# Four weight tiles of two output projections: plain fp32 products in place of three products of high and low parts

## The chip, the cores and the metric

The kernel runs on one core of one Trainium2 chip. The metric is the device time of one execution in microseconds (us), and the lower the better. The time before is the median of three runs.

## What is computed

The reference is a stack of two blocks of two layers on an input of 256 tokens by 1024 features, all in fp32. The first block is a banded attention, an MLP, a recurrent (RG-LRU) layer and an MLP. The second is an RWKV-7 time mix and a differential attention. Each of the layers of the second block ends in the same way, and this ending is where the change is:

```python
# layer 0: y is the time mix, layer 1: y is the differential attention
y = y.reshape(B, S, D).astype(xn.dtype) * jax.nn.silu(g)
return y @ w_out                       # w_out is 1024 x 1024: the output projection
...
h = h + rms_norm(y, norm_post[i])
e = p[i] @ ple_w[i]
g = jax.nn.sigmoid(h @ ple_gate[i])
h = h + rms_norm(g * e, ple_norm[i])   # called the embedding step below
```

## The kernel before

**Weights.** All weights are laid out as 73 tiles of 512 columns (or rows), and each tile is four pieces of 128 x 1024 fp32 (512 KB). SP loads the 292 pieces in order into a ring of eight slots (`ring`, line 687); piece m waits until TensorE has used piece m - 8, and TensorE counts the pieces that it has used in `piece_used`. The four tiles of the change are `W_OUT_A`, `W_OUT_A + 1` (pieces 220 to 227) and `W_OUT_B`, `W_OUT_B + 1` (pieces 272 to 279). Behind each pair come the tile of the embedding weights (`W_PLE0` or `W_PLE1`, four plain pieces) and the two gate tiles (eight pieces, split), pieces 232 to 239 and 284 to 291.

**Split products.** Most tiles are multiplied in the reduced fp32r type with a correction. ScalarE rounds the piece to `high_r` (`split_until`, line 868), GpSimd subtracts that from the piece and writes `ring_r` (`low_until`, line 709), and the activations are split in the same way: they are transposed on TensorE into PSUM, ScalarE writes `x_high` (`evacuate_high`, line 268) and VectorE writes `x_low` (`evacuate_low`, line 286). A product of a 128 x 128 and a 128 x 512 block is then three matmuls (high by high, high by low, low by high). The set `PLAIN` names the tiles that are not split. Their product is one fp32 matmul from `ring` itself. The eight tiles of `W_RKVG`, ahead of `W_OUT_A`, are plain already, and so are the two tiles of the embedding weights. Both kinds of product are recorded under line 409.

**Order.** Every engine's program is one hand-written list. `pe_linear` runs a pair of tiles: per tile four pieces, per piece two k blocks by two token tiles, so 16 products a tile and 32 a pair. `hold_clock(bank, n)` (line 203) issues n dummy fp32 matmuls of 128 columns. On ScalarE `split_for(n)` means that all pieces up to 4n + 9 have been split, so ScalarE runs six pieces ahead of the tile at hand, and waits in its program where such a piece has not landed yet. On GpSimd `low_until(4 * W_PLE0)` comes ahead of five DMAs (the embedding inputs pT, four rows of parameters) and that of `lamb` (lines 778, 715 and 782). In the loop over the sixteen heads of the differential attention, ScalarE splits one piece a head (two at the last): from head 10 on these are the pieces of `W_OUT_B`. GpSimd splits them in between its `combine` steps (line 813) and `gate_rows` (line 821).

**The ending of a layer.** TensorE transposes the gated output (instance `T_YA` or `T_OB`), multiplies it with the pair of tiles, and issues 6 dummy matmuls. Then it waits for the squares of the second half (ScalarE, line 1102) and the products with the gain (VectorE, line 1639). It multiplies with the embedding weights (line 2148), transposes h, waits for ScalarE's copy of the embedding (line 1120), issues 9 dummy matmuls and starts the gate tiles. In ScalarE's `out_norm`, `split_for(first + c)` stands ahead of the squares of half c.

Of the kernel before, what the change touches and what calls it, by code (L numbers as in the profile page):

```python
# [14 lines left out]
SEQ, D = 256, 1024  # L15
NT, KT = SEQ // P, D // P
# [8 lines left out]
W_RKVG, W_OUT_A, W_PLE0, W_KVQG, W_OUT_B, W_PLE1, W_TILES = 47, 55, 57, 60, 68, 70, 73  # L25
# [2 lines left out]

REC = ["x0", "x1", "x2", "x3", "x4", "x5", "g0", "x6", "x7", "g1", "y0", "y1", "g2", "g3", "y2", "y3", "y4", "y5", "y6", "y7"]
REC_AT = {name: 4 * W_REC + i for i, name in enumerate(REC)}  # L30
PLAIN = {W_PLE0, W_PLE1} | set(range(W_RKVG, W_RKVG + 8))
PLAIN_PIECES = {REC_AT[f"g{i}"] for i in range(4)} | {4 * n + i for n in PLAIN for i in range(4)}

MLP_TILES = set(range(W_MLP0, W_MLP0 + 16)) | set(range(W_MLP1, W_MLP1 + 16))
# [51 lines left out]
def build(nc, x, w, cols, rows, consts, relt, lora1, lora2, pT, lam, out):  # L86
    with ExitStack() as ctx:
# [3 lines left out]
        def sem(name):  # L91
            return ctx.enter_context(nc.semaphore(name))
# [24 lines left out]
        def shaped(v, dims):  # L117
            if len(dims) < 2:
                return v
            names = "abcd"[:len(dims)]  # L120
            return v.rearrange("p (" + " ".join(names) + ") -> p " + " ".join(names),
                               **{k: d for k, d in zip(names[1:], dims[1:])})

        def view(off, *dims):

            n = int(np.prod(dims))
            assert off + n <= ARENA, (off, dims)
            return shaped(arena[:, off:off + n], dims)

        def place_r(name, off, n):  # L130

            assert off + n <= ARENA
            return nc.alloc_sbuf_tensor_at(name, [P, n], F32R, offset=arena_base + 4 * off, align_bytes=32)[:, :]

        def raw(m, *dims):

            return shaped(ring[:, m % RING, :], dims)
# [4 lines left out]
        def read(v):  # L142

            return v.bitcast(F32)
# [11 lines left out]
        S = 2048  # L156
# [22 lines left out]

        SPLIT_T = {T_H0, T_O, T_H1, T_N2, T_H3, T_YA, T_H6, T_H7, T_OB, T_H8}
        BANK_OF, ACT_BANKS, DVE_BANKS, PREVIOUS, _last = [], [0], [0], [], {}
        for _i in range(T_H8 + 1):
            for _b in range(4):
                bank_ = 4 + _b if _i in SPLIT_T else 3 if _i in (T_K, T_QB) else 6 + _b % 2
                BANK_OF.append(bank_)
                PREVIOUS.append(_last.get(bank_))
                _last[bank_] = len(BANK_OF) - 1
                ACT_BANKS.append(ACT_BANKS[-1] + (_i in SPLIT_T or _b % 2 == 0))  # L190
                DVE_BANKS.append(DVE_BANKS[-1] + (_i in SPLIT_T or _b % 2 == 1))

        def bank_out(eng, g):

            if ACT_BANKS[g + 1]:
                eng.wait_ge(tp_act, ACT_BANKS[g + 1])
            if DVE_BANKS[g + 1]:
                eng.wait_ge(tp_dve, DVE_BANKS[g + 1])
# [41 lines left out]
        def filling(g):  # L240
            return psum[:, BANK_OF[g], :].rearrange("p (j t) -> p j t", j=2)

        def evacuate(eng, inst, b, dst, gain=None):

            g = 4 * inst + b
            eng.wait_ge(tp_filled, g + 1)
            on_act = b % 2 == 0
            assert on_act == (eng is engines["act"])
            if gain is None:
                dd = dst[:, 2 * b:2 * b + 2, :]  # L250
                ins = nc.scalar.copy(dd, filling(g)) if on_act else nc.vector.tensor_copy(dd, filling(g))
            else:
                for j in range(2):
                    k = 2 * b + j
                    if on_act:
                        ins = nc.scalar.activation(dst[:, k, :], filling(g)[:, j, :], ACT.Copy, scale=gain[:, k:k + 1])
                    else:
                        ins = nc.vector.tensor_scalar(dst[:, k, :], filling(g)[:, j, :], gain[:, k:k + 1], None, ALU.mult)
            ins.then_inc(tp_act if on_act else tp_dve, 1)

        def evacuate_high(act, inst, *pairs, between=None):

            for b in range(4):
                g = 4 * inst + b
                act.wait_ge(tp_filled, g + 1)
                for dst, gain in pairs:
                    if gain is None:
                        ins = nc.scalar.copy(dst[:, 2 * b:2 * b + 2, :], filling(g))
                    else:
                        for j in range(2):  # L270
                            k = 2 * b + j
                            ins = nc.scalar.activation(dst[:, k, :], filling(g)[:, j, :], ACT.Copy, scale=gain[:, k:k + 1])  # L272
                ins.then_inc(tp_act, 1)
                if between is not None:
                    between(b)

        def evacuate_low(dve, inst, *triples):

            for b in range(4):
                g = 4 * inst + b  # L280

                dve.wait_ge(tp_act, ACT_BANKS[g + 1])
                for hi, dst, gain in triples:
                    if gain is None:
                        u = slice(2 * b, 2 * b + 2)
                        ins = nc.vector.tensor_tensor(dst[:, u, :], filling(g), read(hi[:, u, :]), ALU.subtract)
                    else:
                        for j in range(2):
                            k = 2 * b + j
                            ins = nc.vector.scalar_tensor_tensor(out=dst[:, k, :], in0=filling(g)[:, j, :],  # L290
                                                                 scalar=gain[:, k:k + 1], in1=read(hi[:, k, :]),
                                                                 op0=ALU.mult, op1=ALU.subtract)
                ins.then_inc(tp_dve, 1)
# [5 lines left out]
        def h_halves(pe, n):  # L299
# [37 lines left out]
        kv_act, kv_dve, roped, lam_sum, lam_exp, comb_ready, o_act, o_sq, o_var, o_root, od_ready, o_taken, rd_ready, b_scaled = (  # L337
            sem(n) for n in ("kv_act", "kv_dve", "roped", "lam_sum", "lam_exp", "comb_ready", "o_act", "o_sq", "o_var",
                             "o_root", "od_ready", "o_taken", "rd_ready", "b_scaled"))
# [12 lines left out]
        XH, XL, XBH, XBL = (shaped(place_r(name, at * S, S), (KT, SEQ)) for name, at in  # L352
                            (("x_high", 10), ("x_low", 11), ("xb_high", 6), ("xb_low", 7)))
        xT2, xTb2 = (XH, XL), (XBH, XBL)

        def junk_at(i):
            return view((5 if i < 6 else 8) * S, NT, D)
# [35 lines left out]
        def transposed(pe, inst):  # L393

            return lambda i: bank_out(pe, 4 * inst + i)

        def pe_piece(pe, n, i, bank, lhs):

            m = 4 * n + i
            for t in range(NT):  # L400
                tt = slice(t * P, (t + 1) * P)
                for j in range(2):
                    k = 2 * i + j
                    if n in PLAIN:
                        pairs = ((lhs[:, k, tt], raw(m, 2, HALF)[:, j, :]),)
# [7 lines left out]
        def pe_chunk(pe, n, c, lhs, banks_free, ready=None):  # L413

            for i in range(4):
                piece_ready(pe, 4 * n + i)
                if ready is not None:

                    ready(i)
                if i == 0 and banks_free is not None:  # L420
                    banks_free(pe, c)
                pe_piece(pe, n, i, 2 * (c % 2), lhs)

        def pe_linear(pe, first, chunks, lhs, banks_free=None, ready=None):
            for c in range(chunks):
                pe_chunk(pe, first + c, c, lhs, banks_free, ready if c == 0 else None)
# [409 lines left out]
        def _(act):  # L836
# [293 lines left out]
                        square_half(ge[:, t, hl], c, t, 2 * e_n + 1)  # L1130
                post_root(i)

            evacuate_high(act, T_YA, (XH, None))
            out_norm(6, W_OUT_A, 0)
            embed(7, W_PLE0, 0, T_H6)

# [37 lines left out]
            for hh in range(HEADS + 2):  # L1174
# [25 lines left out]
                if hh in PAIR_AT2:  # L1200
                    i, which, b = PAIR_AT2[hh][0]
# [8 lines left out]
                    nc.scalar.copy(pt2[:, g % 2, :], psum[:, 6 + g % 2, 0:384]).then_inc(pt_copied, 1)  # L1210
            heads_square(1)
            heads_root(1)
            evacuate_high(act, T_OB, (XH, None))
            out_norm(9, W_OUT_B, 1)
            embed(10, W_PLE1, 1, T_H8)

# [2 lines left out]
        def _(dve):  # L1219
# [36 lines left out]
            for hh in range(HEADS + 3):  # L1256
# [13 lines left out]
                if hh in PAIR_AT and PAIR_AT[hh][0] % 2 == 1:  # L1270
                    i, which, b = PAIR_AT[hh]
# [381 lines left out]
                                                   g_[:, hl].unsqueeze(1).broadcast_to([P, NT, HALF]), ALU.mult))  # L1653
                add_normed(i, 2 * e_n + 1)

            evacuate_low(dve, T_YA, (XH, XL, None))
            out_gain(6, W_OUT_A, 0, "norm_post0")
            dve.wait_ge(h_ready, 6)
            embed_dve(7, 0, T_H6, "ple_norm0")
# [49 lines left out]
            for hh in range(HEADS + 1):  # L1709
# [18 lines left out]
                if hh in PAIR_AT2:  # L1728
                    i, which, b = PAIR_AT2[hh][1]
# [8 lines left out]
            heads_var(1)  # L1738
            heads_norm(1)
            heads_gate(1)  # L1740
            evacuate_low(dve, T_OB, (XH, XL, None))
            out_gain(9, W_OUT_B, 1, "norm_post1")
            dve.wait_ge(h_ready, 8)
            embed_dve(10, 1, T_H8, "ple_norm1")
# [3 lines left out]
        def _(pe):  # L1748
# [32 lines left out]
            for hh in range(HEADS + 3):  # L1781
# [7 lines left out]
                if hh in PAIR_AT:  # L1789

                    i, which, b = PAIR_AT[hh]
# [363 lines left out]

            pe_transposes(pe, T_YA, yN, lambda b: pe.wait_ge(y_ready, b // 2 + 1))
            hold_clock(0, 8)
            pe_linear(pe, W_OUT_A, 2, xT2, None, transposed(pe, T_YA))
            embed_pe(W_PLE0, 0, T_H6)


# [77 lines left out]
            kvqg_out(8)  # L2239
            hold_clock(0, 16)  # L2240
            pe_transposes(pe, T_OB, oD, lambda b: pe.wait_ge(od_ready, b // 2 + 1))
            pe_linear(pe, W_OUT_B, 2, xT2, lambda pe, c: pe.wait_ge(o_taken, 2) if c == 1 else None, transposed(pe, T_OB))
            embed_pe(W_PLE1, 1, T_H8)

def layout(inp):
# [101 lines left out]
```

## Time and profile before

| | before |
|---|---|
| median of 3 runs | 1169.71 us (1169.52 to 1169.93) |
| the profiled execution | 1173.79 us, span 1172.0 us |
| TensorE matmul busy | 1113.3 us, 95% of the span |
| ScalarE busy | 540.0 us, 46% |
| GpSimd busy | 707.8 us, 60% |
| VectorE busy | 475.7 us, 41% |
| mean granted clock of TensorE | 0.988 of full speed |

All steps below are read in the one profiled execution, whose span runs from its first to its last instruction. A time such as 884.16 is that instruction's start in us from the start of the span. A matmul's record is longer than the distance to the next one, since matmuls are pipelined: the cost of one is the distance between starts.

### The profile page before, as it was taken

Reading aid. Unit: us, or ns where it says so; the run is one execution under the profiler, and the core shown is the slowest. Engines: PE = TensorE matmul, PEld = TensorE weight load, DVE = VectorE, ACT = ScalarE, POOL = GpSimd, SP = SyncE. Lnnn points to the kernel's source line nnn. Section 1 sums busy time; section 2 is a strip of 40 time slices with the busy share of each in tenths; the row PEclk is TensorE's granted clock in tenths of the full one; section 3 lists DMA queues with packets and bytes.
Section 4 is the critical chain, followed back from the end, with each engine's and each line's share of the span. In section 5 each row is a group of like instructions: output and inputs, shape, how many; then the busy total and the mean of one; then the engine's idle time right before and its main releaser. Section 6 shows DMA issues by size and latency. Waiting matters only on the chain. (4 is left out here: it accounts for less than half of the span.)

```text
span 1172.0 us, 20965 instructions
## 1 busy us (share of the span) xinstructions
PE 1113.3 (95%) x8956; PEld 925.5 (79%) x8956; DVE 475.7 (41%) x647; ACT 540.0 (46%) x851; POOL 707.8 (60%) x443
## 2 busy tenths in 40 slices
PE   9999999999999899999999999899998889999895
PEld 8788799998899789989984445899847677777864
DVE  1125274333246646521137175535641350233332
ACT  6437364444458755544421151212222564559452
POOL 5975459988947599998820035300034849667770
PEclk9999999999999999999999998999999989999998
DMA  8661455555546355555572443000036425433240
GB/s 319 225 233 55 144 159 184 189 188 189 189 129 212 110 162 183 191 186 193 183 233 72 127 158 110 21 4 4 4 127 236 150 95 183 140 100 120 81 159 36
DMA packets 45852, 169.44 MB, mean 145 GB/s; under 512 B 5088, under 2 KB 5344, under 8 KB 45440
## 3 DMA queue, kind: packets, MB, share of 16 engines
q1 hardware_dynamic: 43312, 159.06, 41.3%
q0 software_dynamic: 2448, 9.05, 2.4%
q8 instruction: 71, 1.16, 0.4%
q14 instruction: 21, 0.17, 0.0%
HBM read 167.03 MB, written 1.05 MB: 143 GB/s over the span
## 5 line engine op out<-in xcount | busy, mean ns | idle before, releaser
L709 POOL TENSOR_TENSOR ring_r<-ring,high_r 128x512 fp32r<-128x512 f32 (+1 forms) x368 | 636.6, 1763 | 238.9 <-ACT high_r L868 223.8
L868 ACT CAST high_r<-ring 128x1024 fp32r<-128x1024 f32 x248 | 256.2, 1049 | 215.6 <-DMA ring<-w 213.5
L435 PE MATMUL psum<-x_high,high_r 128*128 128x256 f32 x640 | 182.4, 285 | 2.2 <-DVE x_low L290 2.2
L435 PE MATMUL psum<-x_low,high_r 128*128 128x256 f32 x640 | 181.1, 283 | 0.0
L435 PE MATMUL psum<-x_high,ring_r 128*128 128x256 f32 x640 | 181.1, 283 | 0.0
L409 PE MATMUL psum<-high_r,x_high 128*128 128x512 f32 x320 | 127.3, 398 | 2.5 <-POOL ring_r L709 1.5
L612 DVE TENSOR_TENSOR arena<-arena 128x512 f32<-128x512 f32 x32 | 54.8, 1713 | 179.6 <-ACT arena L588 179.5
L435 PEld LDWEIGHTS psum<-x_high,high_r 128*128 128x128 f32 x640 | 122.7, 192 | 3.5 <-issue 1.8
L409 PE MATMUL psum<-high_r,x_low 128*128 128x512 f32 x320 | 124.8, 390 | 0.0
L409 PE MATMUL psum<-ring_r,x_high 128*128 128x512 f32 x320 | 124.6, 389 | 0.0
L435 PEld LDWEIGHTS psum<-x_low,high_r 128*128 128x128 f32 x640 | 122.7, 192 | 0.5
L435 PEld LDWEIGHTS psum<-x_high,ring_r 128*128 128x128 f32 x640 | 122.7, 192 | 0.0
L409 PE MATMUL psum<-ring,arena 128*128 128x512 f32 x256 | 115.2, 607 | 0.0
L654 PE MATMUL psum<-high_r,zz_high 128*128 128x512 f32 x256 | 99.8, 390 | 1.3 <-DVE zz_low L619 1.3
L654 PE MATMUL psum<-ring_r,zz_high 128*128 128x512 f32 x256 | 99.7, 390 | 0.0
L654 PE MATMUL psum<-high_r,zz_low 128*128 128x512 f32 x256 | 99.6, 389 | 0.0
L409 PEld LDWEIGHTS psum<-ring,arena 128*128 128x128 f32 x256 | 49.0, 194 | 60.3 <-issue 60.1
L409 PEld LDWEIGHTS psum<-high_r,x_high 128*128 128x128 f32 x320 | 60.0, 188 | 16.4 <-ACT x_high L272 1.6
L409 PEld LDWEIGHTS psum<-high_r,x_low 128*128 128x128 f32 x320 | 60.1, 188 | 12.9
L409 PEld LDWEIGHTS psum<-ring_r,x_high 128*128 128x128 f32 x320 | 60.1, 188 | 11.8
L203 PE MATMUL psum<-con 128*128 128x128 f32 x500 | 59.4, 276 | 5.0 <-ACT arena L1120 3.2
L203 PEld LDWEIGHTS psum<-con 128*128 128x128 f32 x500 | 57.7, 192 | 6.5 <-ACT arena L1120 3.7
(317 smaller groups left out, 1717.2 us busy)
## 6 DMA issues: line engine op xcount, KB each, us to landing
ring<-w SPq DMA_DIRECT2D x292, 512.0 KB, 3.4
row<-rows POOLq DMA_DIRECT2D x14, 512.0 KB, 7.1
arena<-relt SPq DMA_DIRECT2D x2, 1536.0 KB, 10.6
h<-x SPq DMA_DIRECT2D x1, 1024.0 KB, 5.0
arena<-lora POOLq DMA_DIRECT2D x2, 512.0 KB, 6.8
out<-h SPq DMA_DIRECT2D x1, 1024.0 KB, 4.0
con<-consts SPq DMA_DIRECT2D x1, 529.0 KB, 4.5
arena<-pT POOLq DMA_DIRECT2D x2, 256.0 KB, 4.8
```

The source lines that it names most:

```text
L203: nc.tensor.matmul(psum[:, bank, 0:P], sq, sq, start=True, stop=True)
L409: ins = nc.tensor.matmul(psum[:, bank + t, :], a, b, start=(k == 0 and q == 0), stop=(k == KT - 1 and q == len(pairs) - 1))
L435: ins = nc.tensor.matmul(out, a, b, start=(k == 0 and q == 0), stop=(k == KT - 1 and q == 2))
L612: nc.vector.tensor_tensor(zz[:, u, :], zr[:, u, :], zr[:, u, :], ALU.mult).then_inc(zz_ready, 1)
L654: ins = nc.tensor.matmul(psum[:, 2 * t + half, :], a, b, start=(c == 0 and f == 0 and q == 0), stop=(c == 7 and f == 3 and q == 2))
L709: ins = nc.gpsimd.tensor_tensor(low(m)[:, part], raw(m)[:, part], read(high(m))[:, part], ALU.subtract)
L868: nc.scalar.copy(high(m), raw(m)).then_inc(high_made, 1)
```

## The change

The four tiles join `PLAIN`. Their pieces are no longer split by ScalarE and GpSimd, and each of their products is one fp32 matmul in place of three fp32r ones. The transposed activations `T_YA` and `T_OB` are not split either: ScalarE copies banks 0 and 2, VectorE banks 1 and 3, into `xT_full`, an fp32 view of the memory of `x_high`. The PSUM banks stay as they were.

```diff
-PLAIN = {W_PLE0, W_PLE1} | set(range(W_RKVG, W_RKVG + 8))
+PLAIN = {W_PLE0, W_PLE1} | set(range(W_RKVG, W_OUT_A + 2)) | {W_OUT_B, W_OUT_B + 1}
...
-        SPLIT_T = {T_H0, T_O, T_H1, T_N2, T_H3, T_YA, T_H6, T_H7, T_OB, T_H8}
+        SPLIT_T = {T_H0, T_O, T_H1, T_N2, T_H3, T_H6, T_H7, T_H8}
...
-                bank_ = 4 + _b if _i in SPLIT_T else 3 if _i in (T_K, T_QB) else 6 + _b % 2
+                bank_ = 4 + _b if _i in SPLIT_T | {T_YA, T_OB} else 3 if _i in (T_K, T_QB) else 6 + _b % 2
...
+        xT_full = view(10 * S, KT, SEQ)
...
-            evacuate_high(act, T_YA, (XH, None))
+            for b in (0, 2):
+                evacuate(act, T_YA, b, xT_full)
...
-            evacuate_low(dve, T_YA, (XH, XL, None))
+            for b in (1, 3):
+                evacuate(dve, T_YA, b, xT_full)
...
-            pe_linear(pe, W_OUT_A, 2, xT2, None, transposed(pe, T_YA))
+            pe_linear(pe, W_OUT_A, 2, xT_full, None, transposed(pe, T_YA))
```

The same three edits (ScalarE, VectorE, TensorE) are made for `T_OB` and `W_OUT_B`.

## Rows read from the trace of the kernel before

**Rows 1.** Page, part 1 and part 5: busy us, share, instructions; groups under line 409.

```profile
PE 1113.3 (95%) x8956; PEld 925.5 (79%) x8956; DVE 475.7 (41%) x647; ACT 540.0 (46%) x851; POOL 707.8 (60%) x443
...
L409 PE MATMUL psum<-high_r,x_high 128*128 128x512 f32 x320 | 127.3, 398 | 2.5 <-POOL ring_r L709 1.5
...
L409 PE MATMUL psum<-ring,arena 128*128 128x512 f32 x256 | 115.2, 607 | 0.0
```

**Rows 2.** Timeline of TensorE, plain tiles: start us, us, instruction, count, idle before.

```profile
620.27 13.90 PE L409 MATMUL psum<-ring,arena 128*128 128x512 f32 x32
634.10 7.12 PE L1912 MATMUL psum<-arena 128*64 128x256 f32 x32
...
857.11 20.87 PE L409 MATMUL psum<-ring,arena 128*128 128x512 f32 x48
877.81 1.04 PE L215 MATMUL psum<-con,arena 128*128 128x128 f32 x8
```

**Rows 3.** Timeline of TensorE, the pair W_OUT_A: dummies, first products, end.

```profile
881.39 1.95 PE L203 MATMUL psum<-con 128*128 128x128 f32 x16
884.16 0.47 PE L409 MATMUL psum<-high_r,x_high 128*128 128x512 f32 x1 [0.82 <-DVE x_low L286]
...
906.03 1.50 PE L203 MATMUL psum<-con 128*128 128x128 f32 x12
```

**Rows 4.** Timeline of ScalarE and VectorE at the entry of W_OUT_A.

```profile
878.93 3.87 ACT L868 CAST high_r<-ring 128x1024 fp32r<-128x1024 f32 x4
882.71 2.05 ACT L268 CAST x_high<-psum 128x512 fp32r<-128x512 f32 x4
```

**Rows 5.** Timeline of ScalarE and TensorE, from W_OUT_A's end to the gate tiles.

```profile
906.59 1.04 ACT L868 CAST high_r<-ring 128x1024 fp32r<-128x1024 f32 x1 [9.76 <-DMA ring<-w]
907.82 1.04 ACT L868 CAST high_r<-ring 128x1024 fp32r<-128x1024 f32 x1 [0.19 <-DMA ring<-w]
908.77 0.59 ACT L1102 ACTIVATE arena<-psum 128x512 f32<-128x512 f32 x1
...
910.28 8.80 PE L2148 MATMUL psum<-ring,arena 128*128 128x512 f32 x16 [2.75 <-ACT arena L1102]
...
924.07 0.48 PE L409 MATMUL psum<-high_r,x_high 128*128 128x512 f32 x1
```

**Rows 6.** Timeline, the same stretch behind W_OUT_B.

```profile
1122.61 1.50 PE L203 MATMUL psum<-con 128*128 128x128 f32 x12
1122.81 0.60 ACT L1102 ACTIVATE arena<-psum 128x512 f32<-128x512 f32 x1 [0.99 <-PE psum L409]
1124.32 7.11 PE L2148 MATMUL psum<-ring,arena 128*128 128x512 f32 x16 [0.21 <-ACT arena L1102]
1132.29 1.05 ACT L868 CAST high_r<-ring 128x1024 fp32r<-128x1024 f32 x1 [1.72 <-DMA ring<-w]
1137.24 0.48 PE L409 MATMUL psum<-high_r,x_high 128*128 128x512 f32 x1
```

**Rows 7.** Timeline of GpSimd during W_OUT_A: splits, then the DMAs behind them.

```profile
880.04 10.22 POOL L709 TENSOR_TENSOR ring_r<-ring,high_r 128x512 fp32r<-128x512 f32 x8 [0.72 <-ACT high_r L868]
890.22 0.59 POOL L778 DMA_DIRECT2D arena<-pT  x1
890.81 2.09 POOL L715 DMA_DIRECT2D row<-rows  x4
```

**Rows 8.** Windows: busy us (count) of PE, PEld, DVE, ACT, POOL; granted clock; DMA share; GB/s.

```profile
884.00:888.00 4.00, 3.84 (x17) 3.22 (x18) 1.81 (x4) 0.75 (x2) 4.00 (x5) 1.00 0.00 0
...
900.00:904.00 4.00, 4.00 (x20) 3.30 (x19) 0.00 (x0) 0.00 (x0) 0.00 (x0) 1.00 1.03 411
...
912.00:916.00 4.00, 4.00 (x7) 1.55 (x7) 3.69 (x5) 2.09 (x4) 2.72 (x3) 0.63 0.38 131
```

**Rows 9.** Timeline at the last heads of the attention: TensorE, ScalarE and GpSimd.

```profile
1083.41 6.86 PE L203 MATMUL psum<-con 128*128 128x128 f32 x60
1086.73 2.01 ACT L868 CAST high_r<-ring 128x1024 fp32r<-128x1024 f32 x2
1090.54 0.99 POOL L813 TENSOR_TENSOR arena<-arena 128x384 f32<-128x384 f32 x1 [2.34 <-ACT arena L1187]
1091.59 0.55 PE L2237 MATMUL psum<-con,arena 128*128 128x128 f32 x3 [1.31 <-POOL arena L813]
```

**Rows 10.** Chain that ended last, attention, four products of one piece (start us, us, what).

```profile
1058.40 2.95 PE psum L409 x12
```

More of the change, by code:

```diff
@@ L1212, in _ @@
             heads_root(1)
-            evacuate_high(act, T_OB, (XH, None))
+            for b in (0, 2):
+                evacuate(act, T_OB, b, xT_full)
             out_norm(9, W_OUT_B, 1)
@@ L1740, in _ @@
             heads_gate(1)
-            evacuate_low(dve, T_OB, (XH, XL, None))
+            for b in (1, 3):
+                evacuate(dve, T_OB, b, xT_full)
             out_gain(9, W_OUT_B, 1, "norm_post1")
@@ L2241, in _ @@
             pe_transposes(pe, T_OB, oD, lambda b: pe.wait_ge(od_ready, b // 2 + 1))
-            pe_linear(pe, W_OUT_B, 2, xT2, lambda pe, c: pe.wait_ge(o_taken, 2) if c == 1 else None, transposed(pe, T_OB))
+            pe_linear(pe, W_OUT_B, 2, xT_full, lambda pe, c: pe.wait_ge(o_taken, 2) if c == 1 else None, transposed(pe, T_OB))
             embed_pe(W_PLE1, 1, T_H8)
```

## The prediction

> **What bounds the kernel now.** I read the page's busy shares first: TensorE is busy for 1113.3 of 1172.0 us, every other engine for 60% or less [rows 1]. So a change counts by what it does to TensorE's own stretches and to the few holes between them. I then read the timeline of TensorE over the two pairs of tiles, for the distance between starts and not for the mean of a record. The pair W_OUT_A runs from 884.16 to 906.03, 21.87 us for 96 records without a hole [rows 3], 0.228 us a record. It is bound by TensorE alone. The holes lie around it: 0.82 us ahead of the first product, 2.75 us behind the last [rows 3, 5], and one of 1.31 us at the last heads of the attention [rows 9].
>
> **What one product costs, split and plain.** A split product is three records, 21.87 / 32 = 0.683 us. For a plain one the eight W_RKVG tiles are the measure. The group of plain products has 256 records [rows 1], but eight tiles of 16 products are 128: each plain product leaves two records. The timeline says the same: the first W_RKVG tile, 16 products, stands as 32 records from 620.27 to 634.10, and 24 products stand as 48 records from 857.11 to 877.81 [rows 2]. That is 0.864 and 0.863 us a product. The weights come from the same ring and the activations from SBUF, so I take 0.863 us and no other bound is needed; a mean record of 607 ns [rows 1] is neither the cost of a product nor of a record.
>
> The change is therefore 0.863 - 0.683 = 0.180 us more a product, 32 x 0.863 = 27.6 in place of 21.87 us a pair: +5.7 us for each of two pairs, +11.5 us in all. All of it is on the path, since nothing else is late there.
>
> A sentence on the pages: the Trainium skill, Perfetto Trace Analysis, section Engine Utilization, halves the array's output rate for FP32_LOW_HIGH. Read as the price of a whole fp32 product that would be half a plain price, and the change would gain. The page FP8 and Floating Point Precision, section TensorE Precision Notes, names four passes for true fp32, and the trace agrees with this one: two records for a product, each about twice as long in its distance (0.43 us) as an fp32r record (0.228 us).
>
> **What goes away around the pairs.**
>
> *Entry of W_OUT_A.* ScalarE splits four pieces until 882.8 and only then writes x_high [rows 4]; VectorE's x_low follows, and TensorE, whose dummies end at 883.34 (881.39 + 1.95), starts at 884.16 [rows 3]. Now ScalarE is free at 878.93, copies bank 0 at once, and the products start with the end of the dummies: -0.8 us. The dummies themselves stay. The new copies of VectorE (banks 1 and 3) are needed one and three pieces later, 3.5 us and more, and cost nothing. If they were late they would cost at most the 0.8 us again.
>
> *Entry of W_OUT_B.* No hole stands there, the products follow the transposes. Nothing is gained: 0.
>
> *Behind W_OUT_A.* ScalarE must split pieces 232 and 233 ahead of the squares of the second half. They landed late: the first cast starts at 906.59 and the second at 907.82, each after a wait for the DMA, and the squares at 908.77 [rows 5]; behind W_OUT_B they start 0.2 us after the last product [rows 6]. Why late: GpSimd splits until 890.2 and only then issues pT and four rows [rows 7]. The DMA engines stood still at 884 to 888 and were full (share 1.03) at 900 to 904 [rows 8]. Now GpSimd has no piece to split there, so it issues these DMAs about 10 us earlier, when the engines are idle; the queue of the pieces is passed by them in a quiet stretch. The pieces also have more time: slot 232 comes free with the fifth piece of the pair and the last product is 3 x 3.45 us behind it, against 3 x 2.73 us. So the squares should start at once, as behind W_OUT_B. The hole also cost clock: in the stretch 912 to 916 the granted clock is 0.63, between the levels of 1.2 and 2.4 GHz, after TensorE had stood for 2.75 us, and the 16 records of the embedding took 8.80 us, against 7.11 us behind W_OUT_B, where the idle time was 0.21 us [rows 5, 6, 8]. From the start of the six dummies to the first gate product it took 924.07 - 906.03 = 18.0 us [rows 5] and behind W_OUT_B 1137.24 - 1122.61 = 14.6 us [rows 6]. I take the second for both: -3.4 us. What is late next is the cast of the last piece that ScalarE splits ahead of its copy of the embedding (1132.29, after a DMA [rows 6]), which both endings have and which doesn't move against the last product. The bounds of this term: 0 if the transfers are as late as before, and -3.6 us if a little more of the second ending's own wait goes too.
>
> *Behind W_OUT_B.* Its two early pieces have the same extra time and caused no wait: 0.
>
> *The last heads.* Eight casts of about 1.0 us leave ScalarE's list from head 10 on, two of them at 1086.73 just ahead of the scaling for which GpSimd's last combine waits [rows 9], and GpSimd loses 16 half pieces of about 1.3 us (10.22 us for eight [rows 7]). TensorE waits 1.31 us for that combine. But ahead of it TensorE has its own 60 dummy records from 1083.41 to 1090.27 (1083.41 + 6.86), and these don't shrink. So of some 8 us that ScalarE saves, 1091.59 - 1090.27 = 1.3 us reach the path: -1.3 us. The bounds are 0 and -2.8 us. The second is for products that were themselves slightly held up: four split products of a piece stand as 2.95 us in the chain [rows 10], where 12 x 0.228 is 2.74 us, which is 0.2 us for each of about seven such heads, 1.5 us in all.
>
> *Elsewhere.* Behind both gate pairs each engine stands as before relative to TensorE: with eight slots in the ring no splitting engine can run further ahead than it does. The two x_low buffers and the casts that go save time on engines that don't bound.
>
> **The sum**, made in the profiled execution: +5.7 + 5.7 - 0.8 - 3.4 - 1.3 = +5.9 us, so 1179.7 us where it took 1173.8. The median of the runs is 4.1 us below that execution, and the trace can't say which waits are shorter in an unprofiled run; I add the same difference to it: 1169.7 + 5.9 = 1175.6 us. If the wait behind W_OUT_A is one of those that were shorter, its term shrinks and the time is higher, so the upper side of the range is the longer one.
>
> **The rivals.**
>
> *The late pieces stay late* (slower still). The DMAs of GpSimd move, but they may meet the transfers of pieces 224 to 227, and what was a queue at 900 could stay one. Then nothing of the 3.4 us comes back: +9.3 us, 1179.0 us. For it: the transfers were issued in the same order before. Against it: the idle stretch at 884 to 888 [rows 8]. Chance 0.16.
>
> *ScalarE was the real bound of the attention* (not slower). The chain that ended last runs through ScalarE from about 1062 to 1090. If TensorE's products there were held back by it and not only lengthened by restarts, the eight casts could come back in full: 8 us in place of 1.3, and the sum would be -0.8 us, 1168.9 us. The place is heads 10 to 15, the price 1.0 us a cast, and it decides once more than 3.6 of the 8 us reach TensorE (5.9 - 2.3). Against it: TensorE shows no wait there up to 1083.41, and the 60 dummies stand between. Chance 0.06, of which 0.04 stays within 0.2%.
>
> *A record is a product* (the change does what its price would promise). Then a pair takes 13.8 us, -8.1 us each, and with the other terms 1169.7 - 16.1 - 5.5 = 1148 us. The counts of rows 1 and 2 speak against it. Chance 0.01.
>
> *A smaller gain is missed*: the other terms come back more than I take, as by the -2.8 us at the heads and the whole of -3.6 us, or a wait appears at a new place, an entry above all. That spans +3.9 to +7.5 us around my sum, and counts as my forecast; a further 0.05 lies at +1.5 to +3 us by several of them together.
>
> **How the numbers follow.** The forecast has 0.72, its own range 1173.6 to 1177.5 us. The range for 8 in 10 takes in the late pieces with a little of their spread: 1173.0 to 1179.6 us. A measurement of this kernel tells about 0.2% (2.3 us) from no change, so slower by more than that begins at 1172.0 us. Slower: 0.72 + 0.16 + most of the rest, 0.90. Within 0.2%: 0.07, from ScalarE as the bound and from several small gains together. Faster: 0.03.
>
> **What would show it.** In the profile of the changed kernel each pair stands as 64 records over 27.6 us; at half of that the third rival is right. The first product of W_OUT_A starts right behind the dummies. The squares behind it start within half a microsecond of the last product, the embedding's 16 records take about 7.1 us at a granted clock of 1.0, and the stretch to the gate tiles is 14.6 us; where it is 18, the late pieces stayed late. The idle time ahead of the last transposes of the attention is gone, and the 60 dummies are followed at once. The prediction is wrong if the stretch from head 10 to the dummies shrinks by more than 2 us, or if a wait appears inside a pair.

## The result, and the profile after

The changed kernel takes 1176.26 us (median of 4 runs, 1174.55 to 1177.11), beside 1169.82 us before: a ratio of 1.0050, with a 95% interval of 1.0033 to 1.0068. Timed again later (e10 below) it is 1176.41 beside 1171.82 us, 1.0042 (1.0026 to 1.0057). So it is slower by about 5 us, 0.4 to 0.5%. The forecast was 1175.6 us, +5.9 us.

The profiled execution took 1175.56 us, span 1173.8 us, where that of before had a span of 1172.0 us. The spans differ by only 1.8 us, and that is misleading: the changed stretch begins with the dummies ahead of W_OUT_A, and they stand at 881.39 in the trace of before [rows 3] and at 878.11 in that of after. Up to there nothing was changed but ScalarE's and GpSimd's splits of W_OUT_A's first pieces and the start of GpSimd's DMAs (pT at 875.11 in place of 890.22, the rows at 877.42 in place of 890.81). In the fourteen traces of this study that point lies anywhere from 876.3 to 881.4. So each stretch below is compared by itself, from landmark to landmark.

Timeline of TensorE after, W_OUT_A to the gate tiles (columns as in [rows 2]; the line numbers of after are 1 to 5 higher):

```profile
878.11 1.95 PE L203 MATMUL psum<-con 128*128 128x128 f32 x16
879.89 10.46 PE L410 MATMUL psum<-ring,arena 128*128 128x512 f32 x24
...
907.36 1.50 PE L203 MATMUL psum<-con 128*128 128x128 f32 x12
909.08 7.11 PE L2153 MATMUL psum<-ring,arena 128*128 128x512 f32 x16 [0.21 <-ACT arena L1103]
...
919.76 3.65 PE L203 MATMUL psum<-con 128*128 128x128 f32 x18 [1.83 <-ACT arena L1121]
...
923.07 0.77 PE L410 MATMUL psum<-high_r,x_high 128*128 128x512 f32 x1
```

The products run from 879.89 to 907.36, 27.47 us, in place of 21.87 [rows 3]. They start 1.78 us behind the start of the dummies, as soon as these end, in place of 2.77. Behind them the embedding starts after 1.72 us, with 0.21 us of idle time, in place of 4.25 us and 2.75 [rows 5]. Then something new: the 18 dummy records ahead of the gate tiles take 3.65 us, not the 2.27 us that they take where the clock is full. The windows of this stretch show the granted clock (columns as in [rows 8]):

```profile
918.00:920.00 2.00, 0.24 (x2) 0.24 (x3) 0.00 (x0) 2.00 (x3) 2.00 (x2) 1.00 0.74 254
920.00:922.00 2.00, 2.00 (x13) 2.00 (x13) 1.70 (x3) 2.00 (x5) 2.00 (x3) 0.60 0.04 14
922.00:924.00 2.00, 2.00 (x10) 1.86 (x10) 0.79 (x2) 1.55 (x2) 2.00 (x3) 0.55 0.00 0
924.00:926.00 2.00, 2.00 (x10) 1.66 (x9) 0.00 (x0) 0.00 (x0) 2.00 (x3) 1.00 0.02 4
```

TensorE stood still for 1.83 us up to 919.76, and for the next four microseconds it has little more than half of its clock: the level of 1.2 GHz, and then 2.4 GHz again.

ScalarE behind W_OUT_A, after: both casts of the early pieces (232 and 233) are done 2.1 us ahead of the last product, and the squares follow it by 0.2 us.

```profile
900.45 1.05 ACT L869 CAST high_r<-ring 128x1024 fp32r<-128x1024 f32 x1 [5.13 <-DMA ring<-w]
904.24 1.04 ACT L869 CAST high_r<-ring 128x1024 fp32r<-128x1024 f32 x1 [2.74 <-DMA ring<-w]
907.56 0.60 ACT L1103 ACTIVATE arena<-psum 128x512 f32<-128x512 f32 x1 [2.28 <-PE psum L410]
```

The last heads, after, TensorE, GpSimd and VectorE:

```profile
1082.15 6.86 PE L203 MATMUL psum<-con 128*128 128x128 f32 x60
...
1085.38 0.99 POOL L814 TENSOR_TENSOR arena<-arena 128x384 f32<-128x384 f32 x1 [5.89 <-ACT arena L1189]
...
1096.42 1.09 PE L215 MATMUL psum<-con,arena 128*128 128x128 f32 x8 [1.12 <-DVE arena L1710]
...
1095.14 1.22 DVE L1710 SCALAR_TENSOR_TENSOR arena<-arena 128x1024 f32<-128x1024 f32 x1
```

The combine ends at 1086.4, while TensorE's 60 dummies run until 1088.9. The wait ahead of the second half of the last transposes, and the same gate step of VectorE (line 1706 there, 1710 here), in the trace of before:

```profile
1098.09 1.74 DVE L1706 SCALAR_TENSOR_TENSOR arena<-arena 128x1024 f32<-128x1024 f32 x1
1099.88 1.09 PE L215 MATMUL psum<-con,arena 128*128 128x128 f32 x8 [1.80 <-DVE arena L1706]
```

The step was 0.5 us longer there, beside GpSimd's splits, and TensorE waited for it in both kernels: 1.80 us before, 1.12 us after.

All stretches side by side, each the difference of two starts in the timeline of TensorE (us). "Last transposes" are the second eight (1099.88 before, 1096.42 after), and "last product" stands for the start of the dummies behind it:

| stretch | before | after | difference |
|---|---|---|---|
| dummies ahead of W_OUT_A to its first product | 2.77 | 1.78 | -1.0 |
| the 32 products of W_OUT_A | 21.87 | 27.47 | +5.6 |
| last product to the gate tiles | 18.04 | 15.71 | -2.3 |
| gate tiles to the 60 dummies | 159.34 | 159.08 | -0.3 |
| 60 dummies to W_OUT_B's last transposes | 16.47 | 14.27 | -2.2 |
| those transposes and the 32 products of W_OUT_B | 22.73 | 28.40 | +5.7 |
| last product to the gate tiles | 14.63 | 14.20 | -0.4 |
| from there to the end of the span | 34.76 | 34.74 | 0.0 |
| sum | | | +5.1 |

The -0.3 and -0.4 us are no larger than what differs between traces in places that a run leaves alone: the ending behind W_OUT_B takes 14.20 to 14.78 us wherever its clock holds, and the stretch from the gate tiles to the 60 dummies 158.7 to 159.5 us in twelve of the fourteen traces.

### The profile page after: what moved, and what is told of

Same layout as the page of the kernel before. It is cut to its first block and busy times, and to the rows that moved or that the text cites. A ratio compares the mean times of both kernels' runs of the same rounds, so it can differ in the third digit from the quotient of the medians.

```text
span 1173.8 us, 20765 instructions
## 1 busy us (share of the span) xinstructions
PE 1119.2 (95%) x8892; PEld 911.4 (78%) x8892; DVE 474.6 (40%) x643; ACT 524.8 (45%) x831; POOL 664.4 (57%) x411
## 3 DMA queue, kind: packets, MB, share of 16 engines
HBM read 167.03 MB, written 1.05 MB: 143 GB/s over the span
## 5 line engine op out<-in xcount | busy, mean ns | idle before, releaser
L710 POOL TENSOR_TENSOR ring_r<-ring,high_r 128x512 fp32r<-128x512 f32 (+1 forms) x336 | 592.9, 1796 | 195.6 <-ACT high_r L869 179.7
L869 ACT CAST high_r<-ring 128x1024 fp32r<-128x1024 f32 x232 | 240.7, 1051 | 223.6 <-DMA ring<-w 223.1
L410 PE MATMUL psum<-ring,arena 128*128 128x512 f32 x384 | 169.3, 599 | 0.0
L410 PEld LDWEIGHTS psum<-ring,arena 128*128 128x128 f32 x384 | 72.6, 191 | 89.3 <-issue 89.1
L410 PE MATMUL psum<-high_r,x_high 128*128 128x512 f32 x256 | 102.5, 400 | 1.7 <-POOL ring_r L710 1.5
L410 PE MATMUL psum<-high_r,x_low 128*128 128x512 f32 x256 | 99.9, 390 | 0.0
L410 PE MATMUL psum<-ring_r,x_high 128*128 128x512 f32 x256 | 99.8, 390 | 0.0
L620 DVE TENSOR_TENSOR zz_low<-arena,zz_high 128x512 fp32r<-128x512 f32 x32 | 64.1, 2002 | 1.1
L410 PEld LDWEIGHTS psum<-high_r,x_high 128*128 128x128 f32 x256 | 48.2, 188 | 13.0 <-ACT x_high L272 1.6
L655 PEld LDWEIGHTS psum<-high_r,zz_high 128*128 128x128 f32 x256 | 48.1, 188 | 11.2 <-issue 1.5
```

The lines of the kernel that those rows point to most:

```text
L410: ins = nc.tensor.matmul(psum[:, bank + t, :], a, b, start=(k == 0 and q == 0), stop=(k == KT - 1 and q == len(pairs) - 1))
L620: nc.vector.tensor_tensor(zl[:, c % 2, u, :], zz[:, u, :], read(zh[:, c % 2, u, :]), ALU.subtract).then_inc(z_low, 1)
L655: ins = nc.tensor.matmul(psum[:, 2 * t + half, :], a, b, start=(c == 0 and f == 0 and q == 0), stop=(c == 7 and f == 3 and q == 2))
L710: ins = nc.gpsimd.tensor_tensor(low(m)[:, part], raw(m)[:, part], read(high(m))[:, part], ALU.subtract)
L869: nc.scalar.copy(high(m), raw(m)).then_inc(high_made, 1)
```

## The experiments

The spread of the runs is larger than the first three runs of before suggested: 87 later runs of it, on three chips, took 1167.4 to 1175.6 us. The intervals are therefore about 0.3% wide, and the verdicts below rest on the stretches of the traces as much as on the medians. Each median stands beside that of the kernel before on the same chip. The ratios and their intervals are not quotients of these medians, and in e6 the two differ most (0.9965, by the medians 0.9980).

### e1: plain products, the splits kept

```diff
-PLAIN_PIECES = {REC_AT[f"g{i}"] for i in range(4)} | {4 * n + i for n in PLAIN for i in range(4)}
+PLAIN_PIECES = {REC_AT[f"g{i}"] for i in range(4)} | {4 * n + i for n in PLAIN - {W_OUT_A, W_OUT_A + 1, W_OUT_B, W_OUT_B + 1} for i in range(4)}
...
-                            ins = nc.gpsimd.tensor_tensor(low(m)[:, part], raw(m)[:, part], read(high(m))[:, part], ALU.subtract)
+                            to = high(m) if m // 4 in PLAIN else low(m)
+                            ins = nc.gpsimd.tensor_tensor(to[:, part], raw(m)[:, part], read(high(m))[:, part], ALU.subtract)
```

> The changed kernel, but the sixteen pieces of the four tiles are still split by ScalarE and GpSimd (GpSimd writes its result over high_r, nobody reads it), and TensorE waits for it as before. So the products are plain and the relief of the two engines is taken out. Theory (TensorE pays 5.6 us a pair, the rest comes back through the lists of ScalarE and GpSimd): the last heads give nothing back, the entry of W_OUT_A still gives 0.7 us since x_low is not needed, the stretch behind W_OUT_A gives 0 to 2.3 us: 1178.1 to 1180.4 us, 8.2 to 10.5 us over the kernel before. Rival (the relief of the engines is worth nothing and the unprofiled difference is all products): the same time as the changed kernel, 1176.3 us, within 1 us.

Measured: 1180.45 beside 1171.40 us, 1.0072 (1.0050 to 1.0094): +8.4 us, between 5.9 and 11 us, and +9 us by the medians. That is in the range of the theory; the stretches below say more than the four runs. The pairs take 27.54 and 28.39 us, as in the changed kernel. The last heads take 16.49 us, as before the change, with their wait:

```profile
1083.54 6.86 PE L203 MATMUL psum<-con 128*128 128x128 f32 x60
1091.72 0.55 PE L2243 MATMUL psum<-con,arena 128*128 128x128 f32 x3 [1.31 <-POOL arena L815]
...
1100.03 1.09 PE L215 MATMUL psum<-con,arena 128*128 128x128 f32 x8 [1.81 <-DVE arena L1711]
```

So the splits are what had cost the 2.2 us there: before has the same two waits (1.31 and 1.80 us), after has 0 and 1.12 us. The entry takes 2.01 us: even behind the four casts the products lose only 0.2 us, since no x_low is waited for. Behind W_OUT_A the embedding starts after 1.72 us although GpSimd issues its DMAs at 889 us, 6.7 us behind the first product, where before had issued them 6.1 us behind it. The second early piece's cast ends 1.4 us ahead of the end of the products. That was the first sign against my reason for the late pieces.

### e2 and e3: one pair alone

Each undoes the edits of the other pair: its tiles leave `PLAIN`, its activations are split again, and `pe_linear` takes `xT2`.

> Only W_OUT_A is plain, W_OUT_B as before. Theory: +5.6 for the products, -1.0 at the entry, -2.3 to -3.4 behind the pair: 1171.0 to 1172.1 us. Rival (the stretch behind W_OUT_A was late only in the profiled execution of the kernel before): +4.6 us, 1174.4 us.

> Only W_OUT_B is plain, W_OUT_A as before. Theory: +5.6 for the products, -1.3 at the last combine and -0.9 in VectorE's two steps that ran beside GpSimd's splits (1.74 us before, 1.22 us after): +3.4 us, 1173.2 us. Rival (the casts alone count, VectorE's steps do not reach the path): +4.3 us, 1174.1 us.

e2: 1.0031 (1.0015 to 1.0046), 1174.72 us. e3: 1.0035 (1.0019 to 1.0051), 1175.07 us. The two together, 1.0066, are a little over the whole change and agree with it within their intervals. The medians can't tell theory and rival apart in either case. For e2 the intervals give +1.8 to +5.4 us, where the theory had +1.2 to +2.3 and the rival +4.6; for e3 +2.2 to +6.0 us, with +3.4 and +4.3. The traces can, for the changed stretches: e2 has 1.79, 27.47 and 1.71 us for entry, products and start of the embedding, and keeps the last heads at 16.48 us; e3 keeps 2.76, 21.89 and 3.88 us at W_OUT_A and has 14.26 and 28.40 us at the heads and W_OUT_B. Each gain belongs to the pair that it was put down to. The rival of e2, that the wait behind W_OUT_A was one of a single execution, is refuted by e3 and by e8 below, which leave that ending as it was: TensorE stands for 2.39 and 2.61 us ahead of the embedding there.

### e4: the DMAs held back

```diff
             low_until(4 * W_PLE0)
-            used(pool, W_RKVG + 7)
+            used_piece(pool, 4 * W_OUT_A + 2)
             pool.dma_start(pT_sb, pT[:, 0]).then_inc(lor_landed, 16)
```

> The changed kernel, with GpSimd's six DMAs (pT, rows, lamb) held back until TensorE has used the third piece of W_OUT_A, about 890 us, where the kernel before issued them. Theory (their early issue is what brings pieces 232 and 233 in time): the squares wait again and the stretch from the end of W_OUT_A to the gate tiles is about 18 us, some 2.3 us longer: 1178.6 us. Rival (the slower plain products alone give the pieces the time): the stretch stays at 15.7 us or less and the time at 1176.3 us.

1175.43 beside 1171.40 us, 1.0026 (1.0013 to 1.0039): no slower than the changed kernel. GpSimd and ScalarE in its trace:

```profile
891.00 0.60 POOL L779 DMA_DIRECT2D arena<-pT  x1 [94.29 <-PE psum L410]
...
905.35 1.04 ACT L869 CAST high_r<-ring 128x1024 fp32r<-128x1024 f32 x1 [9.69 <-DMA ring<-w]
906.61 1.05 ACT L869 CAST high_r<-ring 128x1024 fp32r<-128x1024 f32 x1 [0.22 <-DMA ring<-w]
907.90 0.60 ACT L1103 ACTIVATE arena<-psum 128x512 f32<-128x512 f32 x1 [0.25 <-PE psum L410]
```

The pieces are late again, 5 us later than in the changed kernel (905.35 against 900.45), and it doesn't matter: the slower products end at 907.70, and the casts are done at 907.66. That is only just in time, but the DMAs stand 10.8 us behind the first product here, later than in before (6.1 us) and in e1 (6.7 us, 1.4 us to spare). The rival holds. The theory is refuted for the changed kernel: the time that the plain products take is enough by itself.

### e6: the DMAs moved up in the kernel before

```diff
-            low_until(4 * W_PLE0)
+            low_until(4 * W_OUT_A + 4)
             used(pool, W_RKVG + 7)
             pool.dma_start(pT_sb, pT[:, 0]).then_inc(lor_landed, 16)
...
             pool.dma_start(lamb, bass.AP(lam.tensor, 0, [[0, P], [64, 4], [1, 64]])).then_inc(lam_landed, 16)
+            low_until(4 * W_PLE0)
```

> The kernel before with one move: GpSimd issues pT, the rows and lamb behind the splits of the first four pieces of W_OUT_A and ahead of those of the last four; all products stay split. Theory (the DMAs' late issue made pieces 232 and 233 late): the squares start within 0.3 us of the last product and the stretch to the gate tiles falls from 18.0 to between 14.6 and 15.7 us: -2.3 to -3.4 us, 1166.4 to 1167.5 us. Rival (split products leave too little time for the pieces, or the stretch is late only under the profiler): 1169.8 us.

1168.77 beside 1171.15 us, ratio 0.9965 (0.9949 to 0.9980). All products are split, and yet:

```profile
876.33 0.59 POOL L778 DMA_DIRECT2D arena<-pT  x1
...
902.15 1.05 ACT L869 CAST high_r<-ring 128x1024 fp32r<-128x1024 f32 x1 [1.72 <-DMA ring<-w]
...
903.09 1.50 PE L203 MATMUL psum<-con 128*128 128x128 f32 x12
904.80 7.11 PE L2149 MATMUL psum<-ring,arena 128*128 128x512 f32 x16 [0.21 <-ACT arena L1103]
```

The stretch up to the embedding is 1.71 us in place of 4.25 [rows 5]. By the ratio the kernel is 4.1 us faster (2.3 to 6.0), by the medians 2.4 us: the rival is refuted. So with split products the late issue of the DMAs is the cause, and moving them is enough, if barely: the second cast ends at 903.20, 0.1 us behind the last product. e4 and e6 together: either remedy cures the hole. The change applied both, and had 2.1 us to spare.

### e7: and the casts behind x_high

On top of e6, ScalarE casts the last four pieces of W_OUT_A behind its writes of x_high.

```diff
-                split_until(4 * W_OUT_A + 4 * j + 4)
+                if j == 0:
+                    split_until(4 * W_OUT_A + 4)
...
             evacuate_high(act, T_YA, (XH, None))
+            split_until(4 * W_OUT_A + 8)
```

> The kernel before with GpSimd's DMAs moved up and ScalarE's last four casts of W_OUT_A behind its writes of x_high. Theory: -2.5 us behind W_OUT_A plus part of 1.7 us of clock, and -1.0 us at the entry: -3.6 to -5.2 us against the kernel before. Rival (the entry gives nothing): -2.5 to -4.2 us.

1166.63 beside 1171.82 us, 0.9964 (0.9948 to 0.9981). The medians differ by 5.2 us, the interval says 2 to 6 us, and it beats both kernels. The entry is 1.71 us (877.34 to 879.05) in place of 2.77, the 32 products 21.88 us, the embedding starts after 1.71 us: the two gains of the change at W_OUT_A are here without its price.

### e8, e9 and e11: the last two casts

In e8 ScalarE's last two casts of the attention stand ahead of `heads_square(1)`, in e11 behind `heads_root(1)`. e9 is e7 with the edit of e8, e11 is e7 with its own. The diff is that of e11; in e8 and e9 the added last line stands ahead of the two lines above it.

```diff
-                split_until(4 * W_KVQG + 12 + FILLED2[min(hh, HEADS)] + (7 if hh < HEADS else 8))
+                if hh < HEADS:
+                    split_until(4 * W_KVQG + 12 + FILLED2[hh] + 7)
...
             heads_square(1)
             heads_root(1)
+            split_until(4 * W_KVQG + 12 + FILLED2[HEADS] + 8)
```

> The kernel before with one move: ScalarE's last two casts of the attention (the ones at 1086.7) stand behind the last copy of the attention in place of ahead of the last scaling. Theory (they hold up the last combine by 1.3 us, and 60 dummies bound the gain): the wait ahead of the last transposes is gone, -1.3 us, 1168.5 us. Rival (the casts only move to where GpSimd's gate step or the pair W_OUT_B waits for them): 1169.8 us or more.

> The kernel before with both moves and a third: ScalarE casts the last four pieces of W_OUT_A behind its writes of x_high in place of ahead of them. Nothing is plain that was not. Theory: -2.3 to -3.4, -1.3 and -0.8 us: 1164.3 to 1165.4 us, faster than both kernels. Rival (the moved casts arrive too late for the second tile of the pair): a wait inside the pair, and no gain over the first move alone.

> As the last, and ScalarE's last two casts of the attention stand behind the square root of the second heads, no longer ahead of their squares. Theory (what spoiled the earlier form was 2 us of casts ahead of the squares, which left TensorE idle for 2.7 us ahead of W_OUT_B's last transposes, and the clock fell): the stretch from the 60 dummies to those transposes is 15.2 us in place of 16.5, the idle time there 1.8 us, and the kernel 1.3 us faster than the one with two moves. Rival (casts so late leave GpSimd behind for the second tile): a wait inside W_OUT_B and no gain.

All three failed in what was expected of the last casts. e8 is slower than before, 1173.23 us, 1.0018 (1.0005 to 1.0031). e9 (1167.80 us) and e11 (1168.66 us) are faster than before, 0.9975 (0.9960 to 0.9989) and 0.9973 (0.9959 to 0.9987), but no faster than e7 without the move; on the same chip e11 is 2.0 us slower than e7. The combine was no longer waited for (the 60 dummies are followed at 6.70 us). But the wait moved to the transposes, and there it cost more. In e8, the second half of the transposes, and the windows around them:

```profile
1098.27 1.97 PE L215 MATMUL psum<-con,arena 128*128 128x128 f32 x8 [2.71 <-DVE arena L1708]
```

```profile
1096.00:1098.00 2.00, 0.00 (x0) 0.00 (x0) 1.97 (x2) 0.23 (x1) 2.00 (x2) 1.00 0.00 0
1098.00:1100.00 2.00, 1.73 (x9) 1.74 (x9) 1.41 (x3) 0.58 (x1) 2.00 (x2) 0.55 0.02 4
```

The two casts (1090.02, 1.99 us) stand ahead of ScalarE's squares, TensorE is idle for 2.71 us, and its clock falls: the stretch of the transposes and the pair takes 24.29 us in place of 22.73. In e11 the casts are out of that chain and the idle time is still 2.68 us. There a step of VectorE on 8 elements, which took 0.17 us in the trace of after, started just behind the first of GpSimd's next splits:

```profile
1087.09 10.91 POOL L709 TENSOR_TENSOR ring_r<-ring,high_r 128x512 fp32r<-128x512 f32 x8
1087.17 1.22 DVE L1694 TENSOR_SCALAR small<-small 128x8 f32<-128x8 f32 x1
```

That split ends at 1088.36 and VectorE's step at 1088.39, 1.05 us later than at 0.17 us; ScalarE's square root (1088.42) and the rest follow. I had ordered two engines and overlooked the third. This explanation of e11 was read, not tested.

### e5: fewer dummies in the changed kernel

```diff
-                        hold_clock(4, 30)
+                        hold_clock(4, 15)
```

> The changed kernel with 15 in place of 30 dummy matmuls ahead of the last transposes of the attention. Theory (since ScalarE lost its casts there, the dummies are what TensorE waits for, not the combine, which ends 2.7 us before them): -2.5 us, 1173.8 us, with a short wait for GpSimd's combine at 1086.4. Rival (the combine moves or the idle time costs clock in the transposes and products behind it): no gain.

1175.90 beside 1171.15 us, 1.0037 (1.0026 to 1.0049). The stretch from the dummies to the transposes fell from 14.27 to 11.89 us, as the theory says, so the dummies did bound the gain at the last heads. That the whole kernel gained these 2.4 us the medians don't show: 4.75 us over before against 4.59 us in e10, on different chips. The theory's 2.5 us for the kernel are thus not shown. In the profiled execution 2.0 of them are given back at the clock: the last stretch to the gate tiles takes 16.22 us in place of 14.20, with 18 dummy records of 3.90 us. Whether the shorter dummies brought that about or it only fell so in this execution stays open.

### e10: the changed kernel again

> The changed kernel as it is, on the chip and beside the same runs of the kernel before as the three others of this call. Theory (clock falls after short idle times come and go with the execution and are the larger part of the spread; the change itself is +5.6 and +5.7 us in the pairs, -1.0 at the entry, -2.5 behind W_OUT_A, -2.2 at the last heads): +4 to +6 us. Rival (the first comparison caught a lucky kernel before): +3 us or less.

1.0042 (1.0026 to 1.0057): slower by 3 to 7 us. The rival (3 us or less) isn't quite shut out by the interval; the stretches stand against it, 27.47 us for the products and 14.26 us at the heads once more.

### e12: the wait filled

On top of e11, three of four groups of transposes of h are issued twice.

```diff
+                if inst in (T_H6, T_H8) and b < 3:
+                    for j in range(2):
+                        for t in range(NT):
+                            ins = nc.tensor.transpose(psum[:, BANK_OF[g], (2 * j + t) * P:(2 * j + t + 1) * P],
+                                                      src[:, t, (2 * b + j) * P:(2 * b + j + 1) * P], ident)
                 ins.then_inc(tp_filled, 1)
```

> As e11_before_three_moves_b, and three of the four groups of transposes of h are issued twice (the same data to the same bank), 1.4 us of TensorE work in the wait of about 2 us that stands ahead of the nine dummies of each embedding step. Theory (the clock falls in some executions since TensorE stands still for 2 us there; with 0.6 us it doesn't): the 18 dummy records take 2.27 us behind both pairs, the spread of the runs is smaller and the median 1 to 2 us lower. Rival (the fall is set by something else than that idle time): dummies of 3.6 us appear again, and the time is the same.

1166.65 us, beside 1168.66 us for e11 on the same chip: 2.0 us less for 1.4 us more work of TensorE, in each of two places. The dummies behind both pairs:

```profile
914.79 2.27 PE L203 MATMUL psum<-con 128*128 128x128 f32 x18 [0.59 <-ACT arena L1127]
...
1128.51 2.27 PE L203 MATMUL psum<-con 128*128 128x128 f32 x18 [0.62 <-ACT arena L1127]
```

The idle time is 0.6 us and the clock held at both. The spread isn't clearly smaller (1164.96 to 1169.07 us, e11: 1166.69 to 1171.58), which is a miss of that expectation. The twelve runs of e12 have a mean granted clock of 0.9885, those of e11 0.9857, so the clock held more in the runs as a whole. e7 and e12 are the fastest kernels of the study; against before e12 has 0.9961 (0.9947 to 0.9975).

## Why the prediction was right

*The price of a product* was right: 0.180 us more a product were forecast, and 27.47 - 21.87 = 5.60 us a pair are 0.175. It held in all six traces with a plain W_OUT_A (27.47 or 27.54 us). Counting the records was the step that mattered: a plain product leaves two of 0.43 us. The rival that took a record for a product is dead. On this point the trace agrees with the Trainium skill, FP8 and Floating Point Precision, section TensorE Precision Notes: "True FP32: 4 passes through PE array"; a product took 0.858 us, 3.8 times the 0.228 us of one fp32r record.

*The entry of W_OUT_A*: -0.8 us forecast, -1.0 measured. The missing 0.2 us are the end of the dummies: the first product starts 1.78 us behind their start, not at the end of their record (1.95 us). The reason, ScalarE's casts, is one of two that each suffice: e7 gets the whole gain from moving them, with x_low still awaited, and e1 keeps them and still has 0.8 us of it, since x_low is gone.

*Behind W_OUT_A*: -3.4 us forecast, -2.3 measured in the trace of after. The wait for the squares went as forecast (-2.5 us), and so did the clock of the embedding (7.11 us for 8.80). But the clock fell one step later, at the dummies ahead of the gate tiles, and took 1.4 us back there. That this place could lose its clock I had not seen, since it kept it twice in the trace of before. In e4 it kept it, and the stretch was 14.07 us, a gain of 4.0 us. The size of the term is thus that of the execution: over the six traces with a plain W_OUT_A the stretch took 14.1 to 16.2 us, 15.1 on average, and over the three that leave this ending as it was (before, e3, e8) 16.8 to 20.0 us, 18.3 on average. The cause that I named first (the DMAs issued earlier) was sufficient, as e6 shows, but not needed: e4 takes it away and loses nothing. The extra time of the pieces, which I named second, carries it alone.

*The last heads*: -1.3 us forecast, -2.2 measured. The 60 dummies were the bound of the first part, as the prediction says and e5 shows; it came to 1.5 us, again 0.2 us more than by the end of their record. The missing 0.7 us are VectorE's. The prediction didn't list the wait of 1.80 us ahead of the second half of the transposes, and took the transposes to follow the dummies by a fixed distance. But VectorE's gate step shrank from 1.74 to 1.22 us when GpSimd had nothing left to split, and a step of 8 elements ahead of it from 0.34 to 0.17 us. So the entry of W_OUT_B, put at 0 with "No hole stands there, the products follow the transposes", had a hole one step further ahead, and 0.7 us of it went. e1, with the splits kept, has the old stretch again (16.49 us). The Trainium skill, SBUF — State Buffer, section SBUF: two separate sides, says of the port pair that VectorE and GpSimd share that it is an exclusive lock where a VectorE operation has two SBUF inputs and GpSimd's reads SBUF. The gate step has two, the split reads SBUF, and the trace agrees: in before a split ends at 1098.75 and the gate step, started at 1098.09, ends 1.1 us behind it, as in all nine traces with splits at this place.

*The sum*: +5.9 us forecast, +5.1 us by the stretches, +4.6 to +6.4 us by the medians. That it came so near is in part luck: behind W_OUT_A 1.1 us less came back in the trace of after than forecast, at the last heads 0.9 us more. That ScalarE was the real bound of the attention is refuted: with eight casts fewer, the stretch from the gate tiles to the dummies moved by 0.3 us. Two figures of the prediction don't add up, and the forecast doesn't rest on them: that rival would decide once 4.9 of the 8 us reach TensorE, 3.6 beyond the 1.3 already counted, and 7.5 us above the median is 1177.2 and not 1177.5 us.

*What the prediction missed* was how little an execution of this kernel repeats another one. It carried a difference of 4.1 us between the profiled execution and the median as if it belonged to the kernel. The medians of before in the later runs were 1171.15 to 1171.82 us, about halfway to that execution. The places where the clock falls, and the point at which the changed stretch begins (876.3 to 881.4), show that the difference is largely of the execution.

## What to carry to other kernels

Price a choice of number format by the distance between starts, and count the records of a product by the loops of the code: here a plain fp32 product took 0.858 us where three fp32r matmuls took 0.683, and the relief of two other engines paid back some 6 of the 11.3 us in the traces, a part of it within their spread. Only what had been late on TensorE's path came back. Then look whether that relief can be had without the price: moving six DMAs and four casts gave the gains of W_OUT_A and a kernel 4 to 5 us faster than before, where the change is 5 us slower. And before taking work out of one engine's list, look at what its neighbours' steps will then run beside.

## What the runs showed of the hardware

**Short idle times cost clock, now and then.** The 18 dummy records ahead of the gate tiles stand behind an idle time of 1.2 to 2.3 us, in two places, in all thirteen traces other than e12's. They took 2.27 us in 13 of 26 cases and 2.9 to 3.9 us in the other 13. The idle time alone doesn't decide: 1.83 us was followed by 3.65 us in after, 2.12 us by 2.27 us in e9. But the cases that lost the clock had 1.8 to 2.25 us of idle time, those that kept it 1.2 to 2.2 us. The longer waits lost it more often still: ahead of W_OUT_B's last transposes 2.7 us cost it in all four traces that have it (e8, e9, e11, e12), and ahead of the embedding 2.75 and 2.61 us cost it in before and e8, while 2.39 us did not in e3. The same happened at other places, e.g. in e4 behind idle times of 1.30 and 0.87 us:

```profile
993.68 1.06 PE L226 MATMUL psum<-con,arena 128*128 128x128 f32 x8 [1.30 <-issue]
995.62 1.09 PE L2200 MATMUL psum<-arena 64*128 64x256 f32 x2 [0.87 <-DVE arena L238]
...
998.51 0.63 PE L410 MATMUL psum<-high_r,xb_high 128*128 128x512 f32 x1
998.94 0.63 PE L410 MATMUL psum<-ring_r,xb_high 128*128 128x512 f32 x1
...
1003.61 0.40 PE L410 MATMUL psum<-high_r,xb_low 128*128 128x512 f32 x1
1003.84 0.39 PE L410 MATMUL psum<-high_r,xb_high 128*128 128x512 f32 x1
```

The distance between these records is 0.43 us up to 1002.35 and 0.23 us behind it, half the clock for some six microseconds. In the trace of before the same 24 records took 5.68 us in the chain, here 8.23. Three or four such places, each lost or kept, are enough for most of the spread of 8 us between the runs. The runs say the same: of the 87 of before, the 19 with a mean granted clock of 0.990 or more took 1168.7 us on average, the 40 with 0.987 or less 1173.0 us. That the clock makes up all of the spread was not shown. Filling one idle time with harmless work (e12) held the clock at it, in both of its places in the one execution profiled.

**VectorE beside GpSimd.** The second gate step of 1024 elements took 1.74 us beside GpSimd's splits, in nine traces, and 1.22 us without them, in the other five; the split that came behind it took 2.3 us in place of 1.3. The step of 8 elements took 0.17 us with GpSimd idle. In the nine traces it took 0.34 to 1.22 us, and each time it ended 0.02 to 0.03 us behind the instruction that GpSimd was running when it started, whatever that was. On a path that waits for VectorE, work of GpSimd is not free even where nobody waits for GpSimd.
